# Rotary embedding in the window attention: half-head copies on ScalarE in place of a product with a turning matrix

## What is computed

```
half = HEAD_DIM // 2
x1, x2 = xf[..., :half], xf[..., half:]
return concatenate([x1 * c - x2 * s, x2 * c + x1 * s])      # c = cos, s = sin of the token's angles
```

## Time and profile before

| what | value |
|---|---|
| median of 3 executions | 1451.29 us (1450.57 to 1452.48) |
| profiled execution | 1450.95 us, of which the span of its trace is 1449.2 us |
| TensorE busy | 1398.1 us, 96% of the span |
| VectorE, ScalarE, GpSimd busy | 981.4, 824.7, 575.6 us |
| mean granted clock of TensorE | 0.991 |

### The profile page before, as it was taken

How to read it: one execution, slowest core, us unless ns; L and a number is a source line. 1 busy time by engine, 2 the same in 40 slices (tenths; PEclk the granted TensorE clock), 3 DMA queues, 4 the chain that set the end, 5 groups by cost and what they waited for, 6 DMA issues and landing times.

```text
span 1449.2 us, 27974 instructions
## 1 busy us (share of the span) xinstructions
PE 1398.1 (96%) x11062; PEld 1310.0 (90%) x11062; DVE 981.4 (68%) x1302; ACT 824.7 (57%) x1179; POOL 575.6 (40%) x192
## 2 busy tenths in 40 slices
PE   5999999999999999999999999999999898999997
PEld 3899888999999999999999998999997757899997
DVE  3312554666889987859899977665665684765665
ACT  4632354555778856567888465545544474555543
POOL 2443334365422222453222233655654201465562
PEclk9999999999999999999999999999999999999999
DMA  7784565345344445674444455655545401544550
GB/s 283 270 313 185 222 234 204 146 176 187 123 172 171 173 175 200 252 275 162 170 166 169 162 204 219 233 203 208 224 177 223 186 30 59 198 181 175 188 187 30
DMA packets 39144, 272.09 MB, mean 188 GB/s; under 512 B 4436, under 2 KB 5588, under 8 KB 6414
## 3 DMA queue, kind: packets, MB, share of 16 engines
q1 hardware_dynamic: 39054, 270.81, 49.8%
HBM read 269.73 MB, written 1.06 MB: 187 GB/s over the span
## 4 chain that ended last, share of the span: by engine, by line
PE 86%; DVE 5%; ACT 4%; DMA 2%; POOL 1%; issue 1%; SPq 0%; DVEq 0%; ACTq 0%
PE ps L1776 22%; PE ps L1777 22%; PE ps L1778 22%; PE ps L616 9%; PE ps L1910 3%; ACT whi L785 2%; POOL wlo L743 1%; DMA raw<-w_dram 1%; PE ps L1813 1%; PE ps L2244 1%; DVE wlo L1205 1%; PE ps L2232 1%; DMA mv<-b_forget_dram 1%; PE ps L2066 1%; PE ps L2064 1%
## 5 line engine op out<-in xcount | busy, mean ns | idle before, releaser
L743 POOL TENSOR_TENSOR wlo<-raw,whi 128x1024 fp32r<-128x1024 f32 (+1 forms) x183 | 573.4, 3136 | 849.2 <-ACT whi L785 849.1
L785 ACT ACTIVATE whi<-raw 128x2048 fp32r<-128x2048 f32 x183 | 349.3, 1910 | 415.2 <-PE ps L1778 233.5
L1205 DVE TENSOR_TENSOR wlo<-raw,whi 128x1024 fp32r<-128x1024 f32 (+1 forms) x183 | 288.0, 1574 | 325.0 <-ACT whi L785 324.4
L1776 PE MATMUL ps<-h_hi,whi 128*128 128x256 f32 x1248 | 360.2, 289 | 4.8 <-POOL wlo L743 4.8
L1777 PE MATMUL ps<-h_lo,whi 128*128 128x256 f32 x1248 | 354.6, 284 | 0.0
L1778 PE MATMUL ps<-h_hi,wlo 128*128 128x256 f32 x1248 | 354.3, 284 | 0.0
L1776 PE MATMUL ps<-g_hi,whi 128*128 128x256 f32 x1040 | 298.4, 287 | 5.8 <-POOL wlo L743 2.6
L1777 PE MATMUL ps<-g_lo,whi 128*128 128x256 f32 x1040 | 294.9, 284 | 0.0
L1778 PE MATMUL ps<-g_hi,wlo 128*128 128x256 f32 x1040 | 294.8, 283 | 0.0
L1776 PEld LDWEIGHTS ps<-h_hi,whi 128*128 128x128 f32 x1248 | 240.9, 193 | 13.3 <-issue 12.8
L1777 PEld LDWEIGHTS ps<-h_lo,whi 128*128 128x128 f32 x1248 | 241.0, 193 | 0.5
(11 more groups left out here) (270 smaller groups left out, 1958.7 us busy)
## 6 DMA issues: line engine op xcount, KB each, us to landing
raw<-w_dram SPq DMA_DIRECT2D x247, 1024.0 KB, 4.8
brev<-w_dram SPq DMA_DIRECT2D x2, 1024.0 KB, 6.8
gates<-w_dram SPq DMA_DIRECT2D x2, 1024.0 KB, 7.7
xlat<-xT_dram SPq DMA_DIRECT2D x1, 1024.0 KB, 4.9
brev<-bias_rows SPq DMA_DIRECT2D x1, 1024.0 KB, 8.9
brev<-ctxT_dram SPq DMA_DIRECT2D x1, 1024.0 KB, 10.2
sra<-w_dram SPq DMA_DIRECT2D x1, 1024.0 KB, 7.2
mqk<-w_dram SPq DMA_DIRECT2D x1, 1024.0 KB, 6.7
```

Of the source, the lines that this page charges most:

```text
L743: pool.tensor_tensor(wlo[:, g.slot, part], raw[:, g.slot, part], whi[:, g.slot, part].bitcast(F32), ALU.subtract).then_inc(lo2_done, 1)
L785: act.activation(whi[:, g.slot, :], raw[:, g.slot, :], ACT.Copy).then_inc(hi_done, 1)
L1205: dve.tensor_tensor(wlo[:, g.slot, part], raw[:, g.slot, part], whi[:, g.slot, part].bitcast(F32), ALU.subtract)\
L1776: pe.matmul(out, w[0], x[0], start=start, stop=False, skip_group_check=True)
```

## The change

Instead of multiplying by a matrix that swaps the halves of each head and changes a sign, ScalarE copies blocks of 32 rows out of PSUM to the 32 rows beside them, with scale -1 or +1 (times `DH ** -0.5` for queries). Four such copies, of 32 x 512 numbers each, make one turned tile. The first multiplication of `rope` then reads this tile from SBUF instead of PSUM. The five products `turn` and the matrix `rot` in the loaded tables go away (64 KB less in one load).

Query tiles 0 and 3 get other banks: 6 and 7 in place of 0 and 4. The four copies of tile 3 are split over the loop's ScalarE steps n = 2 and n = 3, `rope_q(3)` moves from n = 2 to n = 4, `q_hi(3)` from n = 3 to n = 5, and `q_lo(3)` from n = 4 to n = 6. TensorE's waits for turned tiles now stand ahead of `wscores(0)`, `wscores(1)` and `wout(1)`.

```diff
@@ ScalarE
-            Q_BANKS = (0, 1, 2, 4)
+            Q_BANKS = (6, 1, 2, 7)
+            def turned_halves(out, bank, scale, done, rows=range(0, P, DH // 2)):
+                for r in rows:
+                    other = r ^ DH // 2
+                    ins = act.activation(out[r:r + DH // 2], ps[other:other + DH // 2, bank, :].rearrange("p (a t) -> p a t", a=2),
+                                         ACT.Copy, scale=-scale if r < other else scale)
+                if rows[-1] == P - DH // 2:
+                    ins.then_inc(done, 1)
+            def last_query_tiles(rows):
+                turned_halves(q_rot[:, 6:8, :], Q_BANKS[3], DH ** -0.5, qrot_done, rows)
...
                 if i == 0:
+                    turned_halves(k_all[:, :, 0:T], 0, 1.0, krot_done)
...
                     act.activation(q_raw[...], ps[:, Q_BANKS[i - 2], :], ACT.Copy, scale=DH ** -0.5).then_inc(q_sb, 1)
+                    if i < 5:
+                        turned_halves(q_rot[...], Q_BANKS[i - 2], DH ** -0.5, qrot_done)
...
                 turned(n - 1)
-                if n == 3:
+                if n in (2, 3):
+                    last_query_tiles(range(DH * (n - 2), DH * (n - 1), DH // 2))
+                if n == 5:
                     q_hi(3)
@@ VectorE
-            def rope(out, raw_, bank, done):
-                order.mark(dve.tensor_tensor(out, ps[:, bank, :].rearrange("p (a t) -> p a t", a=2), sin, ALU.mult))
+            def rope(out, raw_, done):
+                order.mark(dve.tensor_tensor(out, out, sin, ALU.mult))
...
-                if n == 2:
+                if n == 4:
                     rope_q(3)
...
-                if n == 4:
+                if n == 6:
                     q_lo(3)
@@ TensorE
-            pe.wait_ge(s_late, 16)
-            pe.wait_ge(kv_sb, 2)
-            turn(k_raw, 4, krot_done)
...
             def beside_third():
-                turn_q(1)
...
+                pe.wait_ge(qrot_done, 2)
                 wscores(0)
             def beside_last():
-                turn_q(2)
+                pe.wait_ge(qrot_done, 3)
...
-            features(Slab(PLACE["qkv", 2]), 0, H)
+            features(Slab(PLACE["qkv", 2]), 6, H)
...
-            features(Slab(PLACE["qkv", 3]), 1, H, between=lambda: turn_q(0))
+            features(Slab(PLACE["qkv", 3]), 1, H)
             features(Slab(PLACE["qkv", 4]), 2, H, between=beside_third)
-            pe.wait_ge(k_ready, 1)
-            features(Slab(PLACE["qkv", 5]), 4, H, between=beside_last)
+            features(Slab(PLACE["qkv", 5]), 7, H, between=beside_last)
...
             def wout(i):
                 pe.wait_ge(wt_sb, 2 * i + 2)
+                if i == 1:
+                    pe.wait_ge(qrot_done, 4)
...
             wscores(2)
-            turn_q(3)
             for n in range(H2):
```

More of the change, by code:

```diff
@@ L333, in build @@
         rope_cs = g_flat[:, late:late + 2 * T].rearrange("p (a t) -> p a t", a=2)
-        rot = g_flat[:, late + 2 * T:late + 2 * T + P]
-        wmask = g_flat[:, late + 2 * T + P:late + 2 * T + 3 * P].rearrange("p (a k) -> p a k", a=2)
+        wmask = g_flat[:, late + 2 * T:late + 2 * T + 2 * P].rearrange("p (a k) -> p a k", a=2)
         less_sink = tiny[:, 48:64]
@@ L721, in _ @@
                     sp.wait_ge(br_drained, 6)
-                    sp.dma_start(g_flat[:, late:late + 2 * T + 3 * P], io["tables"]).then_inc(s_late, 16)
+                    sp.dma_start(g_flat[:, late:late + 2 * T + 2 * P], io["tables"]).then_inc(s_late, 16)
             for k in range(0, KT, 2):
@@ L1136, in _ @@
                 if i == 0:
-                    act.activation(k_raw, ps[:, 0, :], ACT.Copy).then_inc(kv_sb, 1)
+                    act.activation(k_raw, ps[:, 0, :].rearrange("p (a t) -> p a t", a=2), ACT.Copy).then_inc(kv_sb, 1)
+                    turned_halves(k_all[:, :, 0:T], 0, 1.0, krot_done)
                 elif i == 1:
@@ L1141, in _ @@
                     act.activation(q_raw[:, 2 * (i - 2):2 * (i - 2) + 2, :], ps[:, Q_BANKS[i - 2], :], ACT.Copy, scale=DH ** -0.5).then_inc(q_sb, 1)
+                    if i < 5:
+                        turned_halves(q_rot[:, 2 * (i - 2):2 * (i - 2) + 2, :], Q_BANKS[i - 2], DH ** -0.5, qrot_done)
                 if i == 3:
@@ L1671, in rope_q @@
                 dve.wait_ge(qrot_done, j + 1)
-                rope(q_rot[:, 2 * j:2 * j + 2, :], q_raw[:, 2 * j:2 * j + 2, :], (5, 6, 7, 6)[j], q_ready)
+                rope(q_rot[:, 2 * j:2 * j + 2, :], q_raw[:, 2 * j:2 * j + 2, :], q_ready)
             def scores_max(n):
@@ L1712, in _ @@
                     dve.wait_ge(krot_done, 1)
-                    rope(k_all[:, :, 0:T], k_raw, 4, k_ready)
+                    rope(k_all[:, :, 0:T], k_raw, k_ready)
                 if i in (3, 4, 5):
@@ L2168, in _ @@
             ada_group("ada_c", 6, 8)
[L2170 to L2174, removed]
             def wscores(n):
@@ L2394 @@
     rope = [np.tile(f(angle).T.astype(np.float32), (4, 1)) for f in (np.cos, np.sin)]
-    rot = np.zeros((P, P), np.float32)
-    for h in (0, DH):
-        for d in range(DH // 2):
-            rot[h + DH // 2 + d, h + d] = -1.0
-            rot[h + d, h + DH // 2 + d] = 1.0
     outside = [np.where(tok[None, :] > tok[:, None], NEG, 0.0), np.where(tok[None, :] < tok[:, None], NEG, 0.0)]
-    tables = np.concatenate(rope + [rot] + outside, axis=1).astype(np.float32)
+    tables = np.concatenate(rope + outside, axis=1).astype(np.float32)
     sel = np.zeros((P, 2 * WIDE), np.float32)
```

## The result

The changed kernel took 1456.21 us (median, 1454.96 to 1459.65), the kernel before on the same chip 1450.99 us: a ratio of 1.0040, 95% interval 1.0029 to 1.0051. One of before's eight executions took 7696 us; without it before's median is 1450.70 us. The change costs 4 to 7 us. I had forecast 1454.4 us in a range up to 1456.8: the result is inside the range and 1.8 us above the forecast. It is also on the slower side of the 0.2% line on which the forecast lay, to which I had given 0.41, against 0.53 for no change that can be told. The profiled execution of after took 1455.21 us, 4.26 us more than before's, and its span is 1453.4 us.

What follows compares the result with a forecast made beforehand. TensorE bounds the kernel, alternating with ScalarE in the loop; 1.8 us won before `wturn(2)` against 4.9 given back by tile 3 makes +3.1 us, 1454.4 us forecast from a median of 1451.29, range 1450.5 to 1456.8.

Steps and rivals of the forecast that it cites:

- 0.2% line: Whole kernel: a change of about 0.2%, 2.9 us, is the least a measurement can tell from none.
- A low stretch that did not occur: Start of the query slabs: low clock falls on the products behind the removed key's turn, so slab 3 ends at 1132.6.
- the sum of 3.1: Whole kernel: 1.8 us won before `wturn(2)`, 4.9 given back by tile 3 in n = 3 to 5, +3.1 us.
- Front: Query slabs up to `wscores(0)`: four 32-row copies at 0.49 us each, TensorE waits 1.5 us, `wscores(0)` starts at 1137.4.
- The rival of the dear copies: 32-row copies cost more than 0.49 us: at 0.6 some 1455.5 us, at 1.02 each 1459.7; chance 0.09.
- `wturn(0)` and `wturn(1)`: Loop start: `wturn(0)` right behind `wscores(2)` at 1150.6, `wturn(1)` at 1156.5 after a wait of 3.7 us.
- The port's part: VectorE beside GpSimd: small steps of `scores_max(1)` wait 1.2 us; `probs(1)`'s scaling is held too, 1.2 us in the sum.
- The rival in which the port doesn't hold: Small steps and scaling run free beside GpSimd: 1450.8 us, or 1453.2 with only the scaling held; chance 0.27.
- The moved tile 3: Loop, n = 3 to 5: `rope_q(3)` ahead of `probs(3)` makes TensorE wait 4.2 us; `wturn(3)` starts at 1168.5.
- Low clock behind the waits: Behind the waits ahead of `wturn(1)` and `wturn(3)`: the clock falls, losing 1.3 us each time.
- The clock stays up: Rival: no low clock behind the two long waits in the loop, 2.6 us less, 1451.8 us; chance 0.11.
- Nothing is given back: Rival: tile 3 hides in ScalarE's gaps in the loop, 7.1 us stay won, 1444.2 us; chance 0.05.

Runs made afterwards that it cites:

- both orders: Changed kernel with tile 3's copies and `q_hi(3)` ahead of `turned(n - 1)`, and `rope_q(3)` behind `probs(3)`: 1448.92 us, 0.9983 of the kernel before.
- filled waits: Changed kernel with products nobody reads in TensorE's waits, 8 ahead of `wturn(1)` and 9 ahead of `wturn(3)`: 1452.51 us, 1.0009 of the kernel before.

## Why the prediction was right, and where it was off

The mechanism of the loop and its places came as forecast. What was off are the sizes of three terms, one that was missing and one that did not occur in this execution; part of the closeness is luck, since they went both ways.

- **A low stretch that did not occur.** "The key's turn ran at the low clock, which will now fall on the products behind it": it did not fall on them in after's profiled execution, where the clock is 1.00 from 1118 to 1122 us. So slab 3 ended at 1131.0 and not at 1132.6. That is a gift of 1.5 us which the sum had not counted on, and no part of the change as I had laid it out. With the stretch in both or in neither the loss is 5.8 us, and the sum of 3.1 is 2.7 too small, not 1.2.
- **Front.** Forecast: a wait of 1.5 us, `wscores(0)` at 1137.4. Measured: 1.38 and 0.66 us around `turn_group`, start at 1136.56, 0.8 us early only because of the gift: from the copy of slab 3 to `wscores(0)` it took 5.5 us, forecast 4.7. The price of a 32-row copy was taken as 0.49 us and measured 0.60 us. Four take 2.39 us, and they follow each other without the overlap that the 128 x 512 copy had:

```profile
1131.71 2.39 ACT L1136 ACTIVATE mqk<-ps 32x512 f32<-32x512 f32 x4
1134.13 0.63 ACT L1160 ACTIVATE m_hi<-state 128x512 fp32r<-128x512 f32 x1
```

  The rival of the dear copies had this as its mild case (0.6 us, 1455.5 us in all), and its price is what came; that rows don't matter and columns do was right (32 rows take as long as 128, 589 against 592 ns).
- **A term that was missing.** Behind the front waits the clock fell to 0.54. Nine profiled executions have these two waits. From the start of `wscores(0)` to that of `wscores(1)` six of them, after's among them, took 8.6 to 8.7 us and two 9.9 and 10.0. The ninth, both orders, kept the clock at 1.00 behind the same waits, the same form as above:

```profile
1138.00:1140.00 2.00, 2.00 (x19) 2.00 (x18) 1.53 (x4) 1.99 (x4) 0.00 (x0) 1.00 0.28 115
```

  It took 8.25 us, of which TensorE waited 1.27 at `wscores(1)` for the turned tile 2; the others waited 0.2. So the low stretch costs 0.4 us in most executions, since it eats a wait that was due anyway, and 1.7 us where it lasts longer. `wscores(1)` came at 1145.18 (forecast 1145.3). That these differences, and the one at 1118 us, make the spread of the changed kernel (spans of 1453.2 to 1457.9 us, with clocks of 0.988 down to 0.983) fits, but was not tested by itself.
- **`wturn(0)` and `wturn(1)`.** Forecast 1150.6 and, after 3.7 us, 1156.5. Measured 1150.22 and, after 3.63 us, 1156.28. The port's part was forecast as 1.2 us for the small steps, and as another 1.2 us in the sum for the held scaling, from bounds only. Measured: 1.21 instead of 0.16, and 2.90 instead of 0.88, of which 1.7 us reach TensorE, since `turned(0)` ended at 1154.53. The rival in which the port doesn't hold is refuted. The rule of the Trainium skill, page "SBUF — State Buffer", section "Who interferes with whom", by which the one of the two that comes second is blocked in full, agrees with this trace for the `tensor_scalar` too: GpSimd's part began 0.11 us ahead of the scalings, which took 2.90 us beside it and 0.88 us without it.
- **The moved tile 3.** Forecast: `wturn(2)` ends at 1163.1, a wait of 4.2 us, `wturn(3)` at 1168.5. Measured: 1162.87, 4.45 us, 1168.44. This step carries the loss, as the two orders show.
- **Low clock behind the waits: the term that was furthest off.** I charged 1.3 us for each of the two stretches, from before's one. Behind the second wait the turn took 0.9, the scores 0.6 and the output product 0.8 us longer: 2.4 us (behind the first it was 1.45). I had counted only the turn and the scores; here `wout`, which is twice as long, was reached at the low clock too. So `wscores(8)` came at 1179.47, not 1178.4, which is in number the whole difference between the +3.1 us of the forecast and the +4.3 us of the profiled execution. That it is so in number is luck, for up to `wturn(3)` the gift of 1.5 us stood against dearer copies, the held scaling and the front's low stretch. The medians differ by 5.2 us and the ratio says 5.8; the gift accounts for this as well as the front's low stretch, and no run tells the two apart.
- **The clock stays up** was refuted by the rows behind both long waits; its price of 2.6 us was too low, as the filled waits show (3.9 us). **Nothing is given back** was refuted for the changed kernel as it stands. Its mechanism is real, though: with two orders changed the copies hide in ScalarE's gaps, and the kernel is 0.17% faster than before. "They share VectorE's queue, in this order" was the reason against it, and an order can be changed.

## What to carry to other kernels

When a step moves from one engine to another, what decides is where it stands in that engine's queue: put it behind the instruction that the bound engine waits for next, and into a gap in which its engine waits anyway. A wait on TensorE costs more than its length, since the work behind it may run at half speed; price that with the work that stands behind it, not with what stood behind another wait. Before a VectorE step comes beside a GpSimd one, see in a trace whether it stands there: here steps with two inputs in SBUF and scalings in SBUF did, a multiplication from PSUM (0.68 us) and a reduction from PSUM that began just ahead of it (1.22 us) did not. Remember that a held part falls on something else. And before two single traces are compared, look at the clock in the stretches that the change doesn't touch: here 1.5 us lay there.

## What of the hardware I had not expected

- **Short waits are enough to lower the clock, sometimes.** Two waits of 1.38 and 0.66 us with 0.6 us of small passes between them left the clock at 0.54 (1138 to 1140 us of after). The same two waits were followed by a low clock in eight of nine profiled executions and by the full clock in one. A wait for weights near 1117 us, of 1.78 to 2.60 us, was followed by a low clock in 4 of 14, and not by its length: 2.29 us had one, 2.60 us had none. In before, a wait of 1.46 us at 1202.6 us had none either.
- **The low stretch costs by what stands in it**: 1.3 us in before, 2.4 us here behind a wait only 0.7 us longer.
- **A copy of 32 rows costs as much as one of 128**, and four in a row follow at 0.60 us each, while a copy ahead of another kind of instruction gave way after 0.48 us.
- **A step on 128 x 2 numbers can stand for 1.05 us** beside a GpSimd subtraction: its size is no protection, and everything behind it in VectorE's queue stands too.
